# The mixer's tail in another order: the last gate product in halves, the recurrent output projection inside the attention, the attention's projection by token halves

## The reference

```
aq, ak, av, hq, hff, hfb, hi, hg, ga, gh = split_in(h @ w_in)
q, k = rope_2d(q_heads(aq), row, col), rope_2d(kv_heads(ak), row, col)
o_att = window_attention(q, k, kv_heads(av), kc, vc, sink)   # 8 heads of 64, two blocks of 128 queries,
                                                             # 512 keys each: 256 tokens + 256 context
o_h   = hgrn_bidir(...)                                      # gated recurrence, 4 heads of 128, both ways
readout = rmsnorm(hg_merge(o_h), g_hnorm) * silu(hg)
y = (sigmoid(ga) * (o_att @ w_o_attn) + sigmoid(gh) * (readout @ w_o_hgrn)) @ w_out
```

## Time and profile before

| | |
|---|---|
| median of 3 runs | 2303.81 us (2303.65 to 2304.32) |
| the profiled execution | 2306.78 us |
| its span, first to last instruction | 2305.0 us |
| mean granted clock | 0.973 |
| TensorE busy | 2151.0 us, 93% |
| VectorE, ScalarE busy | 1081.2 us, 697.0 us |
| chain of waits | TensorE 58%, issue 36%, VectorE 3%, ScalarE 1%, DMA 1% |
| a 2048 KB load of the ring, issue to landing | 8.0 us (median of 64) |

### The profile page before, as it was taken

The page is one execution under the profiler, slowest core; times in us unless marked ns, Lnnn a source line. Parts: engine busy times, 40 slices in busy tenths (PEclk is TensorE's granted clock), DMA queues, the critical chain, the costliest instruction groups (busy, mean ns, idle before and its releaser), DMA issues.

```text
span 2305.0 us, 27478 instructions
## 1 busy us (share of the span) xinstructions
PE 2151.0 (93%) x11288; PEld 1618.9 (70%) x11288; DVE 1081.2 (47%) x1669; ACT 697.0 (30%) x1101; POOL 60.8 (3%) x98
## 2 busy tenths in 40 slices
PE   5999999999997889999999979999899999799996
PEld 3677778756686759988999864446389988544553
DVE  3333333426353236556645752346367456532463
ACT  3111222323121114444544222124145432222240
POOL 0000000100000000000000200000000002000000
PEclk9999999999998799999999989999999999899999
DMA  9555432132231044534533248889744332588894
GB/s 369 238 218 217 169 110 82 73 120 82 80 130 47 1 146 169 191 146 149 167 126 125 95 177 325 331 356 368 290 149 148 126 129 75 212 346 332 350 388 172
DMA packets 53884, 433.54 MB, mean 188 GB/s; under 512 B 7168, under 2 KB 8448, under 8 KB 17536
## 3 DMA queue, kind: packets, MB, share of 16 engines
q1 hardware_dynamic: 49904, 423.35, 47.5%
q10 hardware_dynamic: 3856, 8.42, 1.0%
HBM read 430.71 MB, written 1.05 MB: 187 GB/s over the span
## 4 chain that ended last, share of the span: by engine, by line
PE 58%; issue 36%; DVE 3%; ACT 1%; DMA 1%; DVEq 1%; POOL 0%; POOLq 0%; SPq 0%; ACTq 0%
PE bank L2729 25%; PE bank L2722 8%; PE bank L3432 5%; PE bank L3430 4%; PE bank L3487 3%; PE bank L3485 2%; PE bank L2666 1%; PE bank L3500 1%; PE bank L2873 1%; PE bank L3356 1%; PE bank L2831 1%; DMA ring<-in_early 1%; PE bank L3449 1%; PE bank L2843 1%; PE bank L3462 1%
## 5 line engine op out<-in xcount | busy, mean ns | idle before, releaser
L2729 PE MATMUL bank<-X_HI,ring_lo 128*128 128x256 f32 x1472 | 269.2, 283 | 2.2 <-issue 2.2
L2729 PE MATMUL bank<-HT_HI,W_HI 128*128 128x512 f32 (+1 forms) x704 | 239.8, 341 | 9.3 <-DVE ring_lo L1768 5.1
L2729 PE MATMUL bank<-HT_HI,ring_lo 128*128 128x512 f32 (+1 forms) x704 | 240.6, 342 | 0.0
L2729 PE MATMUL bank<-HT_LO,W_HI 128*128 128x512 f32 (+1 forms) x704 | 238.5, 339 | 0.0
L2729 PEld LDWEIGHTS bank<-X_HI,ring_lo 128*128 128x128 f32 x1472 | 229.3, 190 | 3.8 <-issue 3.7
L1134 ACT ACTIVATE W_HI<-ring 128x2048 fp32r<-128x2048 f32 x66 | 126.4, 1914 | 294.2 <-PE bank L2729 227.1
L2729 PE MATMUL bank<-HT_LO,ring_lo 128*128 128x256 f32 x736 | 207.8, 282 | 0.0
L1768 DVE TENSOR_TENSOR ring_lo<-ring,W_HI 128x2048 fp32r<-128x2048 f32 x66 | 151.0, 2288 | 54.0 <-ACT W_HI L1134 53.9
L2125 DVE TENSOR_TENSOR ring_lo<-ring,ring_lo 128x2048 fp32r<-128x2048 f32 (+2 forms) x64 | 143.1, 2247 | 41.0 <-ACT ring_lo L1328 39.9
L2729 PEld LDWEIGHTS bank<-HT_HI,W_HI 128*128 128x128 f32 x704 | 133.7, 190 | 36.9 <-issue 17.1
L2729 PEld LDWEIGHTS bank<-HT_LO,W_HI 128*128 128x128 f32 x704 | 133.7, 190 | 16.4 <-issue 0.2
(11 more groups left out here) (547 smaller groups left out, 3594.6 us busy)
## 6 DMA issues: line engine op xcount, KB each, us to landing
ring<-in_early SPq DMA_DIRECT2D x64, 2048.0 KB, 8.0
ring<-in_l_moe_in SPq DMA_DIRECT2D x36, 2048.0 KB, 13.9
ring<-in_l_dense SPq DMA_DIRECT2D x62, 1024.0 KB, 4.9
ring<-in_l_moe_out SPq DMA_DIRECT2D x14, 2048.0 KB, 14.0
slot<-in_l_moe_in SPq DMA_DIRECT2D x10, 2048.0 KB, 11.9
slot_xg<-in_l_moe_in SPq DMA_DIRECT2D x10, 2048.0 KB, 12.0
HT<-in_l_moe_in SPq DMA_DIRECT2D x8, 2048.0 KB, 9.1
ring<-in_l_moe_out SPq DMA_DIRECT2D x14, 1024.0 KB, 9.9
```

Source lines behind the costliest of these rows:

```text
L2729: last = mm(out, a, b, start=start and n == 0, stop=stop and n == 2)
```

## The change

The same arithmetic in another order, except that one projection's products are half as wide and twice as many.

1. The last gate product is split: its first half stays before the readout, after the diagonal scores; its second half comes after the turns of queries and keys. ScalarE's tanh and GpSimd's affine step for it move behind the readout's squares and root.
2. The turns of the readout move behind the second half. VectorE makes `KZ` before it normalises the readout. Banks: `J_KZ` 6 and 3, `J_ORT` 2 and 0.
3. The recurrent output projection is cut in four pieces `recurrent_out(i)`, two in each attention block: one before the first `to_keys`, one after the second. VectorE writes `MERGED` from them (`merge_recurrent`).
4. The second block's scores follow the first block's weighing directly, with the turn of the first block's output (`turn_out(0)`) in their middle.
5. The attention's projection is done for 128 tokens at a time: pieces for the first token half before and after `turn_out(1)`, then those for the second. VectorE adds it to `MERGED` piece by piece, and the output product waits for a piece at a time.

```diff
@@ banks
-        J_ORT = jobs.take(2, 3)
         J_QT = jobs.take(4, 5)
-        J_KZ = jobs.take(6, 7)
-        J_S, J_PT, J_PV, J_OT = [], [], [], []
+        J_KZ = jobs.take(6, 3)
+        J_ORT = jobs.take(2, 0)
+        J_S, J_PT, J_PV, J_OT, J_WOH = [], [], [], [], []
...
+            J_WOH += jobs.take(7, 0)
             J_OT.append(jobs.take(7)[0])
         J_WOA = jobs.take(0, 1, 2, 3)
-        J_WOH = jobs.take(4, 5, 6, 7)
@@ ScalarE
-            gate(7)
             for t in range(2):
                 ps = filled(se, J_O[t])
...
-            emptied(se, J_ORT[1])
             for i in range(2):
                 filled(se, J_QT[i])
                 act(QT[:, 2 * i:2 * i + 2, :], cat(J_QT[i], 2, T), ACT.Copy).then_inc(*free(J_QT[i]))
+            gate(7)
@@ GpSimd
+            for i in range(7):
+                gate(i)
             rstd(3, 2, 4 * P, 2)
+            gate(7)
@@ VectorE
             ve.drain().then_inc(state_ready, 1)
+            for g in range(2):
+                ps = filled(ve, J_KZ[g])
+                for half in range(2):
+                    last = ts(KZ[:, 2 * g + half, :], ps[:, :], col("halves", half), None, ALU.mult)
+                last.then_inc(*free(J_KZ[g]))
             ve.wait_ge(rstd_ready, 2)
...
+            def merge_recurrent(i):
+                ve.wait_ge(gate_ready, 5 + i)
+                filled(ve, J_WOH[i])
+                tt(MERGED[:, 2 * i:2 * i + 2, :], cat(J_WOH[i], 2, T), SGH[:, 2 * i:2 * i + 2, :],
+                   ALU.mult).then_inc(*free(J_WOH[i]))
...
+                merge_recurrent(2 * b)
                 ve.wait_ge(probs_ready, 8 * (b + 1))
...
                     copy(PT[:, 1, :], ps[:, :]).then_inc(*free(J_PT[b][h]))
+                    if h == 1:
+                        merge_recurrent(2 * b + 1)
...
             for i in range(4):
                 filled(ve, J_WOA[i])
                 part = tmp[:, i % 2, :].rearrange("p (a n) -> p a n", a=2)
+                tt(part, cat(J_WOA[i], 2, T), SGA[:, 2 * i:2 * i + 2, :], ALU.mult).then_inc(*free(J_WOA[i]))
+                ve.drain()
+                tt(MERGED[:, 2 * i:2 * i + 2, :], MERGED[:, 2 * i:2 * i + 2, :], part, ALU.add).then_inc(merged_ready, 1)
@@ TensorE
             recurrence(1, gate_piece)
-            gate_piece(7)
             pair_scores(J_DIAG[1], KK, HQ)
+            gate_piece(7, (0,))
             pe.wait_ge(state_ready, 1)
...
                 last.then_inc(*full(J_KZ[g]))
+            gate_piece(7, (1,))
+            for t in range(2):
+                emptied(pe, J_O[t])
+                ps = acquire(pe, J_ORT[t])
+                for m in range(4):
+                    last = tr(ps[:, m * P:m * P + P], ONT[:, t, m * P:m * P + P], ident[:, :])
+                last.then_inc(*full(J_ORT[t]))
...
+            def recurrent_out(i):
+                w = loaded(pe, U_WOH).rearrange("p (k n) -> p k n", k=4)
+                ps = acquire(pe, J_WOH[i])
+                for a in range(2):
+                    last = project(J_WOH[i], ps[:, a * T:(a + 1) * T], w, (2 * i + a) * P, lambda k: ORT[:, k, :], kn=4)
+                last.then_inc(*full(J_WOH[i]))
+                if i == 3:
+                    release(U_WOH)
+
+            def attention_out(i, b):
+                w = loaded(pe, U_WOA).rearrange("p (k n) -> p k n", k=4)
+                ps = acquire(pe, J_WOA[i])
+                for a in range(2):
+                    last = project(J_WOA[i], ps[:, a * T + b * P:a * T + b * P + P], w, (2 * i + a) * P,
+                                   lambda k: OT[:, k, b * P:b * P + P], kn=4)
+                if b:
+                    last.then_inc(*full(J_WOA[i]))
...
+            scores(0, range(HEADS))
+            for b in range(2):
                 out = acquire(pe, J_PV[b])
...
+                if b == 0:
+                    emptied(pe, J_ORT[1])
+                recurrent_out(2 * b)
                 to_keys(0)
-                for h in range(1, HEADS):
+                to_keys(1)
+                recurrent_out(2 * b + 1)
+                weigh(0)
+                for h in range(2, HEADS):
                     to_keys(h)
                     weigh(h - 1)
                 weigh(HEADS - 1)
...
+                if b == 0:
+                    scores(1, range(0, 4))
+                    turn_out(0)
+                    scores(1, range(4, HEADS))
+            emptied(pe, J_OT[0])
+            attention_out(0, 0)
+            attention_out(1, 0)
+            turn_out(1)
+            attention_out(2, 0)
+            attention_out(3, 0)
             emptied(pe, J_OT[1])
...
+            for i in range(4):
+                attention_out(i, 1)
+            release(U_WOA)
             for t in range(2):
                 for half in range(2):
...
                     for k in range(KD):
+                        if not t and not half and k % 2 == 0:
+                            pe.wait_ge(merged_ready, k // 2 + 1)
                         last = mm(ps[:, :], MERGED[:, k, t * P:t * P + P], w[:, k, :], start=k == 0, stop=k == KD - 1)
```

More of the change, by code:

```diff
@@ L1602, in _, with gate @@
             x_rstd(2, 3, 4)
-            for i in range(8):
+            def gate(i):
                 sg = (SGA, SGH)[i // 4][:, 2 * (i % 4):2 * (i % 4) + 2, :]
@@ L2047, in _ @@
                    ALU.mult).then_inc(*free(J_PV[b]))
-            ve.wait_ge(gate_ready, 8)
             for i in range(4):
                 filled(ve, J_WOA[i])
[L2053 to L2056, removed]
                 part = tmp[:, i % 2, :].rearrange("p (a n) -> p a n", a=2)
-                tt(part, cat(J_WOH[i], 2, T), SGH[:, 2 * i:2 * i + 2, :], ALU.mult).then_inc(*free(J_WOH[i]))
+                tt(part, cat(J_WOA[i], 2, T), SGA[:, 2 * i:2 * i + 2, :], ALU.mult).then_inc(*free(J_WOA[i]))
                 ve.drain()
-                last = tt(MERGED[:, 2 * i:2 * i + 2, :], MERGED[:, 2 * i:2 * i + 2, :], part, ALU.add)
-            last.then_inc(merged_ready, 1)
+                tt(MERGED[:, 2 * i:2 * i + 2, :], MERGED[:, 2 * i:2 * i + 2, :], part, ALU.add).then_inc(merged_ready, 1)
             post(4, 0, J_WOUT, 2, YT2, 5)
@@ L2856, in query_piece, with gate_piece @@
                     release(u)
-            def gate_piece(i):
+            def gate_piece(i, halves=(0, 1)):
                 u, w = unit(("ga", "ga2", "gh", "gh2")[i // 2])
@@ L2861, in gate_piece @@
                 ps = acquire(pe, job)
-                for a in range(2):
+                for a in halves:
                     last = project(job, ps[:, a * T:(a + 1) * T], w, (2 * (i % 2) + a) * P, x_only)
-                last.then_inc(*full(job))
-                if i % 2:
-                    release(u)
+                if halves[-1]:
+                    last.then_inc(*full(job))
+                    if i % 2:
+                        release(u)
             def pair_scores(J, k_of, q_of):
@@ L2926, in _ @@
                 last.then_inc(*full(J_O[t]))
[L2927 to L2932, removed]
             emptied(pe, J_AQ[1])
@@ L2949, in _, with scores @@
                 last.then_inc(*full(J_KZ[g]))
[L2950 to L2953, removed]
+            gate_piece(7, (1,))
[5 more added lines that the diff above has]
+                last.then_inc(*full(J_ORT[t]))
+            def scores(b, heads):
+                for h in heads:
                     ps = acquire(pe, J_S[b][h])
@@ L2956, in _, with turn_out @@
                        start=True, stop=True).then_inc(*full(J_S[b][h]))
+            def recurrent_out(i):
[14 more added lines that the diff above has]
+                    last.then_inc(*full(J_WOA[i]))
+            def turn_out(b):
+                emptied(pe, J_PV[b])
+                ps = acquire(pe, J_OT[b])
+                for m in range(4):
+                    last = tr(ps[:, m * P:m * P + P], OTOK[:, b, m * P:m * P + P], ident[:, :])
+                last.then_inc(*full(J_OT[b]))
+            for job in J_QT + J_KZ:
+                emptied(pe, job)
+            scores(0, range(HEADS))
+            for b in range(2):
                 out = acquire(pe, J_PV[b])
@@ L2978, in _ @@
                 weigh(HEADS - 1)
[L2979 to L2983, removed]
-            emptied(pe, J_OT[1])
[L2985 to L2995, removed]
+                if b == 0:
[8 more added lines that the diff above has]
+            attention_out(3, 0)
+            emptied(pe, J_OT[1])
+            for i in range(4):
+                attention_out(i, 1)
+            release(U_WOA)
             for t in range(2):
```

## The result

The changed kernel takes 2265.6 us (four runs, 2265.15 to 2267.47) against 2303.81, the median of the three runs shown before: 38.2 us less. A fourth run of the kernel before, taken beside the changed one, took 2311.43; with it the median of before is 2304.07 and the difference 38.5 us. The ratio, taken over all these runs and not from the two medians (whose quotient is 0.9833), is 0.9825, with a 95% interval of 0.9813 to 0.9837. The forecast was 2261.5, with a range of 2255 to 2275. On two other chips the ratio was 0.9818 (0.9804 to 0.9832) and 0.9832 (0.9818 to 0.9845).

The account below looks back on a forecast made before the run. TensorE's path was taken as the bound, with waits and half clock in the mixer's tail. Step gains summed to 43.15 us, less 0.85 for small waits: 42.3 off 2303.81 gives 2261.5 us, range 2255 to 2275.

Parts of the forecast that it names:

- The bound and the place: TensorE, busy 93% of a 2305.0 us span, bounds the kernel; it is thin in the mixer's tail, some 690 to 860 us.
- The ring: Weight transfers: full from 716 to 808, so no transfer runs on its own clock and all that follows shifts as a whole.
- A: Last gate product to first attention scores: 26.78 us before, 18.0 after, all at full clock; gain 8.8 us.
- The wait on the shared bank: Before the first scores: second readout turn and scores both use bank 0, a new wait of 2.0 us, 1.1 idle.
- some 18 us after the last full gate product's end: Sign to look for in the changed profile: where the first attention scores start.
- C: Softmax to weighing: 6.38 us of ScalarE's exponentials unchanged; two output products almost fill the 4.05 us wait, 0.4 idle; gain 0.
- D to H: First weighing to projections, full clock and waits removed: gains of 8.8, 1.7, 1.35, 3.9 and 2.1 us in turn.
- Rivals 1 and 3: Clock falls in the weighing anyway, 2274.2 us (chance 0.08); clock stays at 0.50 through the tail, 2335 us (0.02).
- I: Projections to output product: 29.96 us before, 15.0 after, with 128 half-width passes at 0.112 us; gain 15.0 us.
- Rival 2: Attention projection: half-width passes cost what full ones do, 13.3 us more, gain 29.0, time 2274.8 us; chance 0.04.
- The 0.85 us taken off for small waits: Deducted from the summed gain of 43.15 us for three or four more waits of 0.25 to 0.3 us between groups.
- the last term: Profiled execution, 2.97 us above the median of before, would become 2264.5; on the median 2303.81 - 42.3 = 2261.5 us.

## Why the prediction was right

- The bound and the place were right: nothing but TensorE's path in the tail mattered, and all that follows shifted as a whole (the output product starts 42.2 us earlier: 42.9 from the tail, less 0.7 by which the tail itself began later; the span ends 41.6 earlier). The ring followed as foreseen: the transfer behind the gate weights was issued at 714.75 and not 705.16, and ScalarE's first rounding still stands 18.6 us behind the output product's start (800.61).
- A's gain was put 0.3 us too high: the scores came 20.1 us after the last level's, where 19.8 had been worked out. The wait on the shared bank was named (1.1 us idle) and found (1.04); moving the readout's turns to other banks took it away. The sign "some 18 us after the last full gate product's end" was misworded: by A's own sum it is 19.8, and 20.1 was measured.
- C held to the hundredth. Two products and two heads' turns fill each softmax wait; the forecast left 0.4 us over, the rows show 0.1 to 0.3 (728.30 + 3.62 to 732.04).
- D to H held within 0.15 us in sum, and their reason, the clock, was shown from both sides: unread work alone brings 14.6 us where it acts and 11.3 in before's tail as a whole, and taking the filling out of the changed kernel loses 8.6 beside the work's 14.3. Rivals 1 and 3 did not happen in any of the three profiles of the changed kernel.
- I held: 0.112 a pass for the half width, as the readout's. Rival 2 is out. By itself the half width costs a little (128 x 0.112 is 14.3 us, 64 full-width passes took 14.03); what pays is that half of the work is ready to fill the wait. That is shown in the rows of single profiles only (2.9 us, 1.5 of it a dip of the clock).
- The 0.85 us taken off for small waits was too much: all deviations in the tail together, A's included, are 0.27.
- Off was the last term, from one profile to the medians. The working took the profiled execution's 2.97 us above the median of before as a fixed offset that the changed kernel would have too, and so put 42.3 us under 2303.81. The changed kernel's profiled execution, 2265.15, is 0.45 below its median instead. That is 3.4 of the 4.1 us by which 2265.6 lies above the forecast; the other 0.7 is that the two profiled executions lie 41.6 apart and not 42.3. All 14 executions of the unaltered changed kernel, from 2263.07 to 2268.12, lie above 2261.5. Three executions of before were at hand, all near 2304; a fourth took 2311.43, and on the other chips they spread from 2301.6 to 2314.4. Against the medians of before on the two other chips (2307.3 and 2307.1) the gain is 42.1 and 39.7. So the gain moves by up to 4 us with which executions of before one compares. What makes these differ was not found.

## What to carry to other kernels

Where TensorE waits some us for another engine and the granted clock behind the wait is 0.50, the wait costs more than its length: price the slow stretch behind it too (here 14.6 us behind 8 us of waiting, of which the tail as a whole kept 11.3), and fill the wait with work that has to be done anyway. Look for that work among what is ready early but queued late, as this projection was. And when a piece is moved into a new place, follow its bank as well as its data: the one wait that the new order added was a bank that two neighbours shared.

## What the runs showed of the hardware that was not expected

- Turns and 64-column passes keep the full clock when they start on it (9.0 of 9.0 us busy at 1.00, twice in one profile), but started at half clock they may stay there for the whole weighing, as in block 0 of before. `732.00:744.00` of the kernel with empty waits has TensorE busy 11.88 of 12 us at 0.50, too. The same work has two paces (9.7 and 18.4 us for a weighing), and what went before it decides at which it starts.
- When the clock comes back in such work differs between executions (near the end of block 0's weighing in one of four profiles of before, not at all there in the others), yet before's tail took 126.1 to 126.2 us in all four; in the odd one that is three differences that cancel.
- Filling the norm's waits kept the clock in one profile and lost it in the other, with 1.1 and 0.9 us of idle time left in both.
